# Hyena layers of a Trainium2 kernel: tokens split four ways, the filter's spectra taken a step ahead

## Chip, core and metric

The kernel runs on one core of a Trainium2 chip, in one launch. The metric is the device time in microseconds (us), the median of three runs. The engines are TensorE (PE), VectorE (DVE), ScalarE (ACT), GpSimd (POOL) and the DMA queues that SyncE (SP) and ScalarE issue.

## What is computed

A decoder of four layers (Hyena, window attention, pooling, Hyena, each with a feed-forward part) on 512 tokens of 1024 features, and behind it a second block with gated delta rule, latent attention and an MLP. The change touches the two Hyena layers alone:

```
def hyena_mixer(xn, ...):
    p = conv3(xn @ w_in + b_in)              # 3 x 1024 features, short convolution over tokens
    x1, x2, v = split(p)
    kf = rfft(hyena_filters(L, ...), axis=0) # 2 orders; taps forward and backward, times a decay,
                                             # divided by sum |k| over all taps
    z = v
    for o, gate in enumerate((x1, x2)):
        z = gate * (irfft(rfft(z, n=2 * L) * kf[:, o])[:L] + fbias[o] * z)
    return z @ w_out + b_out
```

## The kernel before

Each engine has its own program, written out by hand, and the programs meet through semaphores. `Tally` counts tiles in PSUM: four banks `acc` and four banks `aux` go round, and TensorE may open a tile only when the one four back has been drained (`acc_drained`, `aux_drained`). An engine takes its instructions strictly in the order of its program. All numbers are float32; a plain float32 matmul shows as two records in the trace. The large weight products are split in two rounded halves (`z_hi`, `z_lo`, and `out_hi` with the low half of the weights left in `ring_r`): three fast matmuls for one exact one. GpSimd makes the low half of the weights (`low_weights`, L806).

The long convolution is a product of spectra. It goes in four steps, `i = 0..3`: order `o = i // 2` and half `c = i % 2` of the 1024 features (512 each). In one step:

- TensorE makes the taps of the filter for the next step (`taps_of`, L1081, 8 matmuls); ScalarE copies them to `filt`, GpSimd multiplies them by the decay (L818, four instructions).
- TensorE transposes z to tokens in rows (L1036), in four groups of tokens; ScalarE copies them to `u_tm` (L1920).
- `spectra` (L1107): 8 tiles of two matmuls for the signal. Even and odd tokens apart give two tiles whose sum and difference are the two halves of a spectrum: ScalarE copies the even one to `tmpE` (L1965), VectorE adds and subtracts (L2553, L2554) into `U`. Behind them half of the filter's tiles, into `K` (which lies in `xn`).
- VectorE multiplies the spectra (`multiply`, L2563 to L2572): two quarters on 512 elements a partition, and a half on 1024.
- The inverse (L1057): 8 matmuls on 256 columns for each of four tiles of 128 features.
- VectorE scales by the filter's norm `invn`, adds the bias part `zbias` that ScalarE made and multiplies by the gate (L2534, L2536).
- The rest of the filter's spectra, and `magnitudes`: the larger of |fwd + bwd| and |fwd - bwd| (ScalarE L1894, VectorE L2486, L2487), whose column sums (L1097, 16 matmuls with one column) and reciprocal (L2495) give `invn`.

`K` holds one filter alone, so it is overwritten only when its products are done. In the last step the output product begins early: `first_half` (L990 to L992, 48 matmuls) stands on TensorE between the spectra and the inverse, and works on the first four tiles of z, whose low halves VectorE makes with `low_z` (L2491) ahead of that step's spectra. `second_half` (L999 to L1001, 48 matmuls) follows the inverse.

## Time and profile before

| | |
|---|---|
| median of 3 runs | 4452.16 us (4445.99 to 4461.49) |
| span of the profiled execution | 4437.2 us |
| own time of the profiled execution | not on its page; the span is what is shown of it |
| TensorE (PE) busy | 4169.9 us, 94% |
| VectorE (DVE) busy | 2225.3 us, 50% |
| GpSimd (POOL) busy | 1445.5 us, 33% |
| ScalarE (ACT) busy | 1236.0 us, 28% |

The span runs from the first to the last instruction. The busy shares are means over all stages; the Hyena layers' four steps each take some 237 us of the span, twice.

### The profile page before, as it was taken

Reading aid. Unit: us, or ns where it says so; the run is one execution under the profiler, and the core shown is the slowest. Engines: PE = TensorE matmul, PEld = TensorE weight load, DVE = VectorE, ACT = ScalarE, POOL = GpSimd, SP = SyncE. Lnnn points to the kernel's source line nnn. Section 1 sums busy time; section 2 is a strip of 40 time slices with the busy share of each in tenths; the row PEclk is TensorE's granted clock in tenths of the full one; section 3 lists DMA queues with packets and bytes.
Section 4 is the critical chain, followed back from the end, with each engine's and each line's share of the span. In section 5 each row is a group of like instructions: output and inputs, shape, how many; then the busy total and the mean of one; then the engine's idle time right before and its main releaser. Section 6 shows DMA issues by size and latency. Waiting matters only on the chain.

```text
span 4437.2 us, 48379 instructions
## 1 busy us (share of the span) xinstructions
PE 4169.9 (94%) x19126; PEld 3108.9 (70%) x19126; DVE 2225.3 (50%) x3267; ACT 1236.0 (28%) x1725; POOL 1445.5 (33%) x834
## 2 busy tenths in 40 slices
PE   7999999999999699999999999989998999998999
PEld 6656888656788488877557887566666666685887
DVE  6567435365424652465774444556663357404322
ACT  3322212135222322233233222322322224422221
POOL 3311344200344144434123442357574000231343
PEclk9999999999999899999999998989999879999999
DMA  6200232210232123221003222121212121221232
GB/s 181 76 16 23 111 105 88 105 48 28 101 115 77 70 96 118 81 77 67 28 29 131 99 90 68 43 60 31 60 30 57 59 77 60 74 95 62 90 105 76
DMA packets 96913, 333.75 MB, mean 75 GB/s; under 512 B 44336, under 2 KB 47536, under 8 KB 67888
## 3 DMA queue, kind: packets, MB, share of 16 engines
q1 hardware_dynamic: 87968, 311.85, 20.2%
q10 hardware_dynamic: 8720, 18.82, 1.7%
q8 instruction: 152, 2.49, 0.2%
q14 instruction: 73, 0.60, 0.0%
HBM read 317.53 MB, written 13.11 MB: 75 GB/s over the span
## 4 chain that ended last, share of the span: by engine, by line
PE 80%; DVE 14%; ACT 2%; POOL 2%; issue 1%; DMA 0%; SPq 0%; DVEq 0%; ACTq 0%; POOLq 0%
PE bank L903 16%; PE bank L904 16%; PE bank L905 16%; PE bank L1340 5%; PE bank L867 4%; PE bank L1107 3%; PE bank L1057 2%; PE bank L1320 1%; PE bank L1641 1%; PE bank L1081 1%; PE bank L1640 1%; PE bank L1662 1%; PE bank L1572 1%; PE bank L1601 1%; DVE work L2598 1%
## 5 line engine op out<-in xcount | busy, mean ns | idle before, releaser
L782 POOL TENSOR_TENSOR w_lo<-ring,w_hi 128x2048 fp32r<-128x2048 f32 (+2 forms) x200 | 777.2, 3886 | 1509.6 <-ACT w_hi L1777 1483.1
L903 PE MATMUL bank<-x_hi,w_hi 128*128 128x512 f32 x1584 | 618.2, 390 | 7.5 <-POOL w_lo L782 7.5
L905 PE MATMUL bank<-x_hi,w_lo 128*128 128x512 f32 x1584 | 616.9, 389 | 0.0
L904 PE MATMUL bank<-x_lo,w_hi 128*128 128x512 f32 x1584 | 616.7, 389 | 0.0
L1777 ACT ACTIVATE w_hi<-ring 128x2048 fp32r<-128x2048 f32 (+2 forms) x200 | 322.0, 1610 | 712.8 <-PE bank L905 711.9
L903 PE MATMUL bank<-h_hi,w_hi 128*128 128x512 f32 x960 | 373.9, 389 | 0.4
L904 PE MATMUL bank<-h_lo,w_hi 128*128 128x512 f32 x960 | 373.5, 389 | 0.0
L905 PE MATMUL bank<-h_hi,w_lo 128*128 128x512 f32 x960 | 373.4, 389 | 0.0
L903 PEld LDWEIGHTS bank<-x_hi,w_hi 128*128 128x128 f32 x1584 | 297.8, 188 | 70.6 <-POOL w_lo L782 9.2
L905 PEld LDWEIGHTS bank<-x_hi,w_lo 128*128 128x128 f32 x1584 | 297.6, 188 | 62.1
L904 PEld LDWEIGHTS bank<-x_lo,w_hi 128*128 128x128 f32 x1584 | 297.8, 188 | 61.5
L2420 DVE TENSOR_TENSOR x<-bank,x 128x512 f32<-128x512 f32 x72 | 49.8, 692 | 388.7 <-PE bank L905 347.5
L1340 PE MATMUL bank<-xn,ring 128*128 128x512 f32 x496 | 238.8, 620 | 1.4 <-DVE work L2741 1.4
L1107 PE MATMUL bank<-work,tab 128*128 128x512 f32 x512 | 225.8, 599 | 12.7 <-ACT work L1920 11.7
L795 POOL TENSOR_TENSOR ring_r<-ring,merge_hi 128x2048 fp32r<-128x2048 f32 x16 | 73.4, 4588 | 498.8 <-ACT merge_hi L2252 498.8
L903 PEld LDWEIGHTS bank<-h_hi,w_hi 128*128 128x128 f32 x960 | 180.2, 188 | 39.4 <-DVE h_lo L2357 2.1
L905 PEld LDWEIGHTS bank<-h_hi,w_lo 128*128 128x128 f32 x960 | 180.2, 188 | 37.4
L904 PEld LDWEIGHTS bank<-h_lo,w_hi 128*128 128x128 f32 x960 | 180.2, 188 | 37.3
L1107 PEld LDWEIGHTS bank<-work,tab 128*128 128x128 f32 x512 | 97.2, 192 | 131.8 <-issue 125.6
L1848 ACT ACTIVATE xn<-xn 128x512 f32<-128x512 f32 x88 | 55.7, 633 | 456.3 <-DVE xn L2433 456.3
L818 POOL TENSOR_TENSOR work<-work,ring 128x1024 f32<-128x1024 f32 x32 | 76.8, 2432 | 264.1 <-ACT work L1889 264.1
L2433 DVE TENSOR_TENSOR xn<-bank,rstd_t 128x512 f32<-128x512 f32 x88 | 60.9, 692 | 194.0 <-PE bank L905 187.3
(468 smaller groups left out, 7666.1 us busy)
## 6 DMA issues: line engine op xcount, KB each, us to landing
ring<-stream SPq DMA_DIRECT2D x212, 1024.0 KB, 4.8
ring<-stream SPq DMA_DIRECT2D x64, 704.0 KB, 4.0
ring<-stream SPq DMA_DIRECT2D x36, 512.0 KB, 3.6
xn<-first_mods SPq DMA_DIRECT2D x8, 1024.0 KB, 6.9
ring<-stream SPq DMA_DIRECT2D x4, 1088.0 KB, 5.0
bias_rows<-work ACTq DMA_DIRECT2D x1, 4096.0 KB, 46.4
work<-bias_rows ACTq DMA_DIRECT2D x1, 3072.0 KB, 11.2
tab<-tabs ACTq DMA_DIRECT2D x1, 2624.0 KB, 16.8
```

What stands on the lines that cost most here:

```text
L782: nc.gpsimd.tensor_tensor(w_lo[:, j % 2, 0:cols], ring[:, k % RING, 0:cols], w_hi[:, j % 2, 0:cols], ALU.subtract).then_inc(wlo_set, 1)
L795: nc.gpsimd.tensor_tensor(ring_r[:, w, 0:2 * DT * P], ring[:, w, 0:2 * DT * P], merge_whi[j % 2][:], ALU.subtract).then_inc(wlo_set, 1)
L818: nc.gpsimd.tensor_tensor(pair, pair, decay[:, pq:pq + 1, :].broadcast_to([P, 2, 512]), ALU.mult).then_inc(filt_set, 1)
L867: ins = mm(b[:], w[:, at + k, :], rhs[k] if isinstance(rhs, list) else rhs[:, k, :], start=(k == 0), stop=(k == kt - 1))
L903: mm(b[:], hi[:, at + k, :], rhs_hi, start=(k == 0), stop=False)
L904: mm(b[:], hi[:, at + k, :], rhs_lo[:, k, :], start=False, stop=False)
L905: ins = mm(b[:], lo[:, at + k, :], rhs_hi, start=False, stop=(k == kt - 1))
L1057: ins = mm(b[:, 256 * p:256 * (p + 1)], U[:, 4 * ft + 2 * kind + p, ct * P:(ct + 1) * P], inv[kind][:, p, ft, :], start=(j == 0), stop=(j ...
L1107: ins = mm(b[:], fwd[kind][:, p, q, ft * P:(ft + 1) * P], source(kind)[:, 2 * p + q, :], start=(q == 0), stop=(q == 1))
L1340: ins = mm(b[:, 0:TC] if ctx else b[:], w[:, at + k, :], src[:, k, :], start=(k == 0), stop=(k == DT - 1))
L1777: signal(go(w_hi[:, j % 2, 0:cols], ring[:, k % RING, 0:cols], ACT.Copy), whi_set)
L2433: drain(tt_(gate, bank(t)[:], rstd, ALU.mult), t)
```

## The change

Tokens are split four ways (token `4t + r`, `r = 0..3`) instead of two. A cosine or sine sum over one residue is one matmul (`FWD`, 12 blocks of 128x128), and sums and differences on VectorE build the spectrum:

- The signal's spectra are 8 matmuls instead of 16 (`signal_spectra`); VectorE builds four classes from them (`signal_pair`, `four_classes`). The filter's stay at 16, 8 tiles of two (`FILTER_PAIRS`).
- The inverse is 8 matmuls of 128 columns for each tile, in two parts: residues 0 and 2 when `prod_set` counts once, 1 and 3 when it counts again.
- The products are `crossed`, `straight`, `joined` and `folded`: VectorE instructions on 2048, 1536, 1024 and 512 elements, all 512 columns at once in steps 0 to 2, in two halves of 256 columns in step 3. Temporary products lie in `partner` (in `ctmp`), `cross` (in the table, which stays as large) and `cross3`.
- `K` is two buffers (`xn` and the new `spectrum2`). The next filter's spectra are made in the step before, between the products, and its taps one step earlier.
- `magnitudes` is two absolute values on ScalarE and one maximum on VectorE (L2535), which stands behind the products, ahead of the gates; its column sums stand behind the next step's signal spectra. The values lie in `x`, so ScalarE stores `x` to memory when the layer begins and loads it in step 3 (2 MB each).
- The output's first four low halves stand behind step 3's products in VectorE's order.

The diff, cut to what matters:

```
 pe:
+                for i in range(4):
+                    signal_spectra()
+                    if i:
+                        magnitudes()
                     if i < 3:
...
+                        filter_spectra()
+                        turns(i + 1)
                     else:
                         begun = first_half(0) + first_half(1)
...
+                    if i < 2:
+                        taps_of(i, later[1])
                     if i < 3:
...
+                        inverse(open_acc, acc_full, range(4))
+                    else:
+                        inverse(open_aux, aux_full, range(2))
+                        inverse(open_aux, aux_full, range(2, 4))
+                def signal_spectra():
...
+                    for pair in SIGNAL_PAIRS:
+                        for kind, r in pair:
+                            mm(open_aux()[:], fwd[kind, r, 1], u_tm[:, r, :], start=True, stop=True).then_inc(aux_full, 1)
+                def inverse_tile(b, ct, r):
+                    for k in range(2):
+                        ins = mm(b[:, P * r:P * (r + 1)], U[:, INVERSE_SLOTS[r][k], ct * P:(ct + 1) * P], inv[:, r, k, :],
+                                 start=(k == 0), stop=(k == 1))
+                def inverse(tiles_of, full_, cts):
+                    tiles = [tiles_of() for _ in cts]
+                    pe.wait_ge(prod_set, n["prod"] + 1)
...
+                    pe.wait_ge(prod_set, n["prod"] + 2)
 act:
+                    if i == 3:
+                        act.dma_start(x[:], x_keep.rearrange("(k p) t -> p k t", p=P)).then_inc(hy_x_back, 16)
                     if i < 3:
...
+                        magnitudes()
+                        spectra(4)
+                        turned()
+                    if i == 2:
+                        for j in range(2):
+                            high_weights(starts[("hyena", s)] + 18 + j, out_hi[j])
 dve:
+                    signal_pair(0, U[:, 0, :], U[:, 2, :])
...
+                    if i:
+                        norms(c)
                     if i < 3:
+                        whole = slice(0, 512)
+                        four_classes(whole)
+                        filter_pair(next_, 0)
+                        crossed(K[c], whole)
+                        filter_pair(next_, 1)
+                        straight(K[c], whole)
+                        filter_pair(next_, 2)
+                        joined(whole)
+                        filter_pair(next_, 3)
+                        folded(whole)
+                        magnitudes()
+                    else:
+                        for part in (slice(0, 256), slice(256, 512)):
+                            four_classes(part)
...
+                            folded(part)
...
                     if i == 3:
                         for m in range(4):
                             low_z(m)
+            def crossed(ker, cs):
+
+                tt_(partner[:, :, cs], U[:, 1:8:2, cs], ker[:, 1:8:2, cs], ALU.mult)
+                tt_(cross[:, :, cs], U[:, 0:6:2, cs], ker[:, 1:7:2, cs], ALU.mult)
+                step(tt_(cross3[:, :, cs], U[:, 6:7, cs], ker[:, 7:8, cs], ALU.mult))
+            def folded(cs):
+
+                low, high = U[:, 0:4, cs], U[:, 4:8, cs]
+                step(tt_(high, low, high, ALU.subtract))
+                step(stt(low, low, 2.0, high, ALU.mult, ALU.subtract))
+                first, second = U[:, 0:2, cs], U[:, 2:4, cs]
+                step(tt_(second, first, second, ALU.subtract))
+                signal(stt(first, first, 2.0, second, ALU.mult, ALU.subtract), prod_set)
```

The order of TensorE in step 1. L1081 are taps, L1036 transposes, L1107 spectra, L1057 the inverse, L1097 column sums. Before:

```order
L1081 MATMUL bank<-ring,work 128x512 x8
L1036 MATMUL bank<-ident,work 128x128 x16
L1107 MATMUL bank<-work,tab 128x512 x24
L1057 MATMUL bank<-tab,work 128x256 x32
L1107 MATMUL bank<-work,tab 128x512 x8
L1097 MATMUL bank<-ones,work 128x1 x16
```

In the changed kernel L1046 are the signal's spectra, L1143 the column sums, L1133 the filter's, L1037 the transposes of the next step, L1123 taps, L1050 the inverse:

```order
L1046 MATMUL bank<-work,tab 128x512 x8
L1143 MATMUL bank<-ones,x 128x1 x16
L1133 MATMUL bank<-work,tab 128x512 x16
L1037 MATMUL bank<-ident,work 128x128 x16
L1123 MATMUL bank<-ring,work 128x512 x8
L1050 MATMUL bank<-tab,work 128x128 x32
```

Taps and transposes moved behind the filter's spectra, so they stand next to the inverse; the column sums moved from the end of a step to the place behind the signal's spectra of the next.

The order of VectorE at the start of step 3. Before, the low halves L2491 follow the reciprocal L2495, ahead of the signal's pairs (L2553, L2554) and the products:

```order
L2495 RECIPROCAL small_t<-bank 128x4
L2491 TENSOR_TENSOR z_lo<-work,z_hi 128x512 x4
L2553 TENSOR_TENSOR work<-work,bank 128x512
L2554 TENSOR_TENSOR work<-work,bank 128x512
L2553 TENSOR_TENSOR work<-work,bank 128x512
L2554 TENSOR_TENSOR work<-work,bank 128x512
L2563 TENSOR_TENSOR work<-work,xn 128x512
```

In the changed kernel the end of the second half's products (L2638 to L2645) stands ahead of the same low halves, now L2539, and the gates (L2604) follow:

```order
L2638 TENSOR_TENSOR work<-work 128x4x256
L2639 SCALAR_TENSOR_TENSOR work<-work 128x4x256
L2641 TENSOR_TENSOR work<-work 128x2x256
L2642 SCALAR_TENSOR_TENSOR work<-work 128x2x256
L2644 TENSOR_TENSOR work<-work 128x2x256
L2645 SCALAR_TENSOR_TENSOR work<-work 128x2x256
L2539 TENSOR_TENSOR z_lo<-work,z_hi 128x512 x4
L2604 SCALAR_TENSOR_TENSOR work<-bank,small_t,work 128x512
```

The low halves moved from ahead of all of the step's products to behind them. TensorE's order there is unchanged: column sums, `first_half`, inverse, `second_half`.

## Rows read from the trace of the kernel before

**Rows 1.** The page's part 4, by line: shares of the span.
```profile
PE bank L903 16%; PE bank L904 16%; PE bank L905 16%; PE bank L1340 5%; PE bank L867 4%; PE bank L1107 3%; PE bank L1057 2%; PE bank L1320 1%; PE bank L1641 1%; PE bank L1081 1%; PE bank L1640 1%; PE bank L1662 1%; PE bank L1572 1%; PE bank L1601 1%; DVE work L2598 1%
```

**Rows 2.** Stretches of the first Hyena layer: us; busy PE, PEld, DVE, ACT, POOL; clock.
```profile
207.52:269.06 61.54, 56.10 (x193) 34.04 (x193) 40.89 (x51) 16.74 (x25) 9.31 (x5) 0.97 0.11 46
269.06:330.55 61.49, 56.04 (x192) 34.01 (x193) 40.89 (x51) 16.75 (x25) 9.30 (x5) 0.97 0.04 13
330.55:385.02 54.47, 49.63 (x177) 31.12 (x177) 40.89 (x51) 16.01 (x20) 7.49 (x3) 0.95 0.11 44
385.02:445.00 59.98, 55.16 (x194) 38.40 (x195) 47.60 (x51) 16.64 (x22) 11.42 (x3) 0.93 0.05 18
```

**Rows 3.** Timeline of TensorE, second step: start, length, engine, line, operation, count, wait.
```profile
269.06 20.84 PE L1107 MATMUL bank<-work,tab 128*128 128x512 f32 x48 [1.56 <-ACT work L1920]
291.26 7.17 PE L1057 MATMUL bank<-tab,work 128*128 128x256 f32 x32 [1.36 <-DVE work L2572]
...
316.48 3.63 PE L1097 MATMUL bank<-ones,work 128*128 128x1 f32 x32
```

**Rows 4.** Timeline of TensorE at the ends of both Hyena layers and the second's start.
```profile
441.13 0.40 PE L999 MATMUL bank<-z_hi,out_hi 128*128 128x512 f32 x1
...
444.63 0.39 PE L903 MATMUL bank<-z_hi,hyena_hi 128*128 128x512 f32 x1
...
2108.33 4.10 PE L1107 MATMUL bank<-work,tab 128*128 128x512 f32 x9 [1.56 <-ACT work L1920]
...
2343.01 0.39 PE L903 MATMUL bank<-z_hi,hyena_hi 128*128 128x512 f32 x1
```

**Rows 5.** TensorE's groups by form: count, then busy us and mean ns.
```profile
L1662 PE MATMUL bank<-work 128*128 128x128 f32 x384 | 49.2, 280 | 0.0
```

**Rows 6.** Timeline of VectorE in the second step.
```profile
291.24 1.22 DVE L2563 TENSOR_TENSOR work<-work,xn 128x1024 f32<-128x1024 f32 x1
...
300.94 0.69 DVE L2553 TENSOR_TENSOR xn<-work,bank 128x512 f32<-128x512 f32 x1
...
302.26 0.69 DVE L2553 TENSOR_TENSOR xn<-work,bank 128x512 f32<-128x512 f32 x1
...
305.96 2.29 DVE L2487 TENSOR_TENSOR work<-work 128x2048 f32<-128x2048 f32 x1
308.29 0.75 DVE L2534 SCALAR_TENSOR_TENSOR work<-bank,small_t,work 128x512 f32<-128x512 f32 x1
...
309.80 0.75 DVE L2534 SCALAR_TENSOR_TENSOR work<-bank,small_t,work 128x512 f32<-128x512 f32 x1
```

**Rows 7.** Timelines of GpSimd and VectorE: the decay of the second step.
```profile
261.30 9.30 POOL L818 TENSOR_TENSOR work<-work,ring 128x1024 f32<-128x1024 f32 x4 [52.23 <-ACT work L1889]
...
272.82 0.69 DVE L2553 TENSOR_TENSOR work<-work,bank 128x512 f32<-128x512 f32 x1 [13.90 <-PE bank L1107]
```

**Rows 8.** Timelines of GpSimd and VectorE where their instructions overlap.
```profile
163.78 10.51 POOL L818 TENSOR_TENSOR work<-work,ring 128x1024 f32<-128x1024 f32 x4 [2.09 <-ACT work L1889]
...
164.16 2.73 DVE L2480 SCALAR_TENSOR_TENSOR work<-work,vec 128x512 f32<-128x512 f32 x1
...
403.79 4.61 POOL L806 TENSOR_TENSOR ring_r<-ring,hyena_hi 128x2048 fp32r<-128x2048 f32 x1 [15.67 <-ACT hyena_hi L1789]
...
500.08 4.61 POOL L782 TENSOR_TENSOR w_lo<-ring,w_hi 128x2048 fp32r<-128x2048 f32 x1 [3.69 <-ACT w_hi L1777]
...
404.05 4.89 DVE L2563 TENSOR_TENSOR work<-work,xn 128x512 f32<-128x512 f32 x1
...
503.51 0.69 DVE L2433 TENSOR_TENSOR xn<-bank,rstd_t 128x512 f32<-128x512 f32 x1 [3.56 <-PE bank L905]
```

**Rows 9.** Timeline and stretch of TensorE after a wait in the first step.
```profile
239.42 8.86 PE L1057 MATMUL bank<-tab,work 128*128 128x256 f32 x32 [2.53 <-DVE work L2572]
...
239.40:243.00 3.60, 3.58 (x9) 2.89 (x10) 3.48 (x5) 0.00 (x0) 0.00 (x0) 0.53 0.00 0
```

**Rows 10.** DMA issues: count, size, us to landing.
```profile
x_keep<-x SPq DMA_DIRECT2D x1, 2048.0 KB, 8.5
```

More of the change, by code:

```diff
@@ L2544, in hyena @@
                 blk.n += 22
-            def spectra(dst, fts=(0, 1)):
-                for j in range(2 * fts[0], 2 * fts[-1] + 2):
-                    ft, kind = j // 2, j % 2
-                    e = aux.take()
-                    t = full(aux, aux_full)
-                    dve.wait_ge(aux_drained[aux.place(e)], aux.turn(e) + 1)
-                    tt_(dst[:, 4 * ft + 2 * kind, :], tmpE[:, j % 2, :], bank(t, True)[:], ALU.add)
-                    drain(tt_(dst[:, 4 * ft + 2 * kind + 1, :], tmpE[:, j % 2, :], bank(t, True)[:], ALU.subtract), t, True)
-                dve.wait_ge(aux_drained[aux.place(t)], aux.turn(t) + 1)
@@ new lines, in pair_tiles, with filter_pair, signal_pair @@
+            def pair_tiles(j):
+                e = aux.take()
+                t = full(aux, aux_full)
+                dve.wait_ge(aux_drained[aux.place(e)], aux.turn(e) + 1)
+                return tmpE[:, j % 2, :], bank(t, True)[:], t
+            def filter_pair(dst, j):
+                even, odd, t = pair_tiles(j)
+                tt_(dst[:, j, :], even, odd, ALU.add)
+                drain(tt_(dst[:, j + 4, :], even, odd, ALU.subtract), t, True)
+            def signal_pair(j, total, rest, flipped=False):
+                first, second, t = pair_tiles(j)
+                tt_(total, first, second, ALU.add)
+                drain(tt_(rest, second, first, ALU.subtract) if flipped else tt_(rest, first, second, ALU.subtract), t, True)
```

307 lines of the change are left out of this document (154 added, 153 removed).

## The prediction

> **What bounds the kernel now.** I read the chain that ended last first: the matmul lines of TensorE fill it, and the two lines of the transforms hold 3% and 2% of it [rows 1]. So the program waits for TensorE, and an edit in the two Hyena layers shows one for one in the span, if it moves the moment at which TensorE leaves the layer. Next the table of stretches, cut at the first signal spectrum of each of the four steps of the first Hyena layer: 61.5, 61.5, 54.5 and 60.0 us, TensorE busy 56, 56, 50 and 55 of them, VectorE 41, 41, 41 and 48 [rows 2]. TensorE bounds the steps, but VectorE is not far behind: halving TensorE's work can gain only until VectorE's column is reached. The timeline of TensorE in one step shows what lies in it: 24 spectra in 20.84 us, 7.17 us for half of the inverse and 3.63 us of column sums, with a short wait of 1.36 us for VectorE ahead of the inverse [rows 3].
>
> The second layer is a copy of this. It goes from the first signal spectrum at 2108.33 to the end of the first output block at 2343.01, 234.7 us; the first goes from 207.52 to 444.63, 237.1 us [rows 2, 4]. Together 471.8 us.
>
> **TensorE's new work.** A transform matmul on 512 columns costs 20.84/24 = 0.87 us [rows 3]. A step had 24 of them for spectra and 8 more behind the inverse; it now has 8 for the signal (7.0 us) and 16 for the filter (13.9 us). The inverse falls from 32 matmuls of 256 columns to 32 of 128. No such matmul is in this stage; elsewhere 384 records of 128x128 take 49.2 us, 0.13 us each, two records to a matmul [rows 5], so 32 cost 8.3 us for 14.3. The bounds are 7.2 (half of today's 14.3) and 14.3. With column sums (3.6) and eight taps (6.9) TensorE needs some 42 us, transposes included, of each of the first two steps, where it needed 56.
>
> **VectorE's new work.** From the timeline [rows 6]: a pair of sum and difference off a bank takes 302.26 - 300.94 = 1.32 us, an instruction on 2048 elements 2.32 us with its gap, one on 1024 a mean of 9.70/8 = 1.21 us inside a run and 1.25 with a wait behind it, a gate and its product 1.51 us. On 1536 I interpolate 1.76 us. The products of a step were 16 instructions on 512 and 8 on 1024, 20.6 us. They are now: four classes 2 x 2.3, crossed 4.7, straight 4.6, joined 4.7, folded 4.6 and then 4 x 1.23: 28.1 us. Pairs stay at 10.6, gates at 6.0, the maximum drops from 4.6 to 2.3. A step's sum is 47.2 us where it was 42: more work on VectorE, and VectorE becomes the engine that sets the step. No one price here is unknown by more than 1 us.
>
> **What moves under VectorE: GpSimd's instructions.** This decides the sign. GpSimd multiplies the taps by the decay in four instructions, 9.3 us, and today this lies in a hole of VectorE: the decay starts at 261.30 and VectorE stands idle 13.90 us before 272.82 [rows 7]. Where the two do overlap, VectorE's instruction does not run beside GpSimd's: the one at 164.16 takes 2.73 us during the decay, where an instruction of its form and size takes 0.75 us free [rows 6], and the one at 404.05 takes 4.89 us, to the end of the 4.61 us that GpSimd's instruction takes from 403.79, for 0.69 on 512 elements otherwise [rows 6, 8]. An instruction with a bank as operand is untouched: 0.69 us in the middle of a GpSimd instruction [rows 8]. And turns alternate: GpSimd's four decays took 10.51 us there and VectorE got one instruction through between two of them. So each GpSimd instruction costs VectorE 2.73 - 0.75 = 2.0 us (decay) or 4.89 - 0.69 = 4.2 us (weights).
>
> The Trainium skill, GPSIMD Engine Reference, section Specifications, says that GpSimd's SBUF interfaces are shared with VectorE, with contention for instructions with two SBUF inputs. The trace agrees (2.73 against 0.75 us). It does not say who gets the next turn. By alternating turns the sum is the one below; by VectorE always going first, it would be that of the first rival.
>
> In the changed order the taps stand behind the filter spectra and the transposes, whose last bank VectorE frees only after its last filter pair. The decay so begins under the folding: three of its instructions delay the second product signal (6.2 us) and one the maximum (2.0). In the third step there are no taps, but the two output-weight splits are issued at the same place: 8.4 us. Both were free before.
>
> **The chain by steps**, from the first signal spectrum (call it 0), "P" being the end of the folding:
> - P of step 0: signal 6.9 + last pair 1.6, four classes 4.6, four filter pairs 5.3, crossed, straight and joined 14.0, folding 9.5, GpSimd 6.2: 48.1.
> - From P to P in step 1: maximum 2.3 and GpSimd 2.0, gates 6.0, the first two signal pairs 2.6 (they free TensorE's banks), TensorE's last signal tile and column sums 0.87 + 3.63 and 0.5 of latencies, reciprocal 0.2, then again 4.6 + 5.3 + 14.0 + 9.5 + 6.2: 57.7. TensorE's own 42 us are hidden in it.
> - Step 2: the same with 8.4 for 6.2: 59.9. P is at 165.7.
> - Step 3: VectorE does maximum 2.3, waits until the inverse (begun at the first product signal, 2.5 before P) has its first tile at 4.8, gates 6.0, pairs 2.6, sums and latencies 5.0, reciprocal 0.2: 18.6 after P. Then the products in two halves, each 8 instructions on 1024 (9.7), 2 on 768 (1.9), 2 on 256 (0.8), 4 on 512 (2.9): 30.6 for both, and 4.2 for the weight split of GpSimd. Only behind them stand the first low halves of z: 54.1 after P.
> - TensorE's first output blocks wait for these and stand ahead of the last inverse. Before, low halves came first, and the 48 matmuls ((444.63 - 441.13)/15 = 0.233 us each, 11.2 us [rows 4]) lay under the products. Now TensorE is idle some 35 us, then 11.2, with 1.7 for half clock, inverse 8.3, first gates and z 1.5 to 2.0, and the other 48 matmuls 11.2: P + 89.
>
> Sum: 254.7 us a layer, 509.4 for two, against 471.8: +37.6. The start of the layer gives back 0.4 us twice (one maximum of 2.3 for two, one absolute value of 1.9 more). The half clock is from a row: after a wait of 2.53 us [rows 9] the granted clock was 0.53 for 3.6 us, so the lower level of 1.2 GHz, worth 1.7 us [rows 9]; elsewhere TensorE's waits lie in VectorE's shade. The two new copies of x lie beside other work: one like them lands in 8.5 us [rows 10], and its result is wanted only after eleven weight blocks on the way out and after step 3's products on the way back; without the cover 17 us a layer. The issue costs ScalarE half a microsecond. If it slows the first weight blocks I allow 0 to 4 us.
>
> So 4437.2 + 37 = 4474 us of span. The median of the runs, 4452.2, lies 15 us above this span; the profiled execution's own time is not on its page, so I add the same 15: 4489. A difference under 0.3%, 13 us, is about what a measurement of this kernel cannot tell from none.
>
> **Rivals.**
> 1. *GpSimd does not take turns; VectorE runs through.* For it: every overlap in the trace has VectorE arriving second or in short runs. Against it: at 403.79 GpSimd started within VectorE's chain, between two of its instructions. Then 29.0 us a layer go (16.4 of decays, 12.6 of splits); but TensorE's taps, 7 us behind the last pair, then end after the first product signal, the gates wait some 1.5 us for tiles, and the half clock falls on the inverse: 20 net. 4489 - 40 = 4449, the same as before. It decides when less than 1 us of each GpSimd instruction reaches VectorE.
> 2. *Faster: VectorE is fed without a wait too.* One mechanism: the tiles arrive a step ahead, as far as four banks allow, so that loop P to P is VectorE's 47.2. P of step 2 is 48.1 - 6.2 + 94.4 = 136.3, step 3 is 89 - 4.2: 221 a layer, -14.8 each: 4452 - 30 = 4422. Against it: the reciprocal stands in VectorE's order behind the signal pairs and needs column sums that TensorE starts only after the last signal tile; that is 5 us a step by order. It turns faster once stalls sum to less than 25 us a layer; I count 40.
> 3. *Much slower.* Each bank wait of TensorE (about 3.6 and 4 us before the last transposes) brings half clock onto the taps and the inverse, 3.4 us for three steps, and the copies delay weights 4: 4489 + 24 = 4513.
> 4. *The new parts don't shorten TensorE*: inverse at 14.3 instead of 8.3 us. Only step 3 and the end of step 2 show it: +12 a layer at most. 4489 + 24.
>
> **Chances.** The forecast, alternating turns and a last step that serialises, 0.64, own range 4470 to 4503. No turns 0.15. Something between (half the turns, 4469) 0.03. Faster 0.10. Rivals 3 and 4 together 0.08. The range leaves out the faster case and the slowest: 4446 to 4503, 8 in 10. Faster by over 0.3%: 0.11; within: 0.17; slower: 0.72.
>
> **What would show it.** In the new trace: signal spectra some 52, 58 and 63 us apart instead of 61.5, 61.5, 54.5; VectorE's 1024-element foldings of 3.2 us beside GpSimd's decays, and of 5.4 us beside the splits in the third step; TensorE idle about 35 us before the first output block, released by the low half of z; 82 us from the last step's spectra to the end of the first output block where it was 60. I am wrong if the foldings keep 1.2 us, if the output block starts under the products, or if steps 0 to 2 are all near 47.

## The result, and the profile after

The changed kernel takes 4522.84 us (median of four runs, 4507.8 to 4526.19) against 4454.77 for the kernel before in the same session: ratio 1.0150, 95% interval 1.0127 to 1.0173, so 68 us slower. The prediction was 4489 and its range ended at 4503, so the result lies outside it. The direction was right, the size about half of what came.

The page of the changed kernel, busy time by engine and the chain that ended last:

```profile
span 4524.4 us, 48077 instructions
...
PE 4107.8 (91%) x18998; PEld 3083.5 (68%) x18998; DVE 2313.3 (51%) x3227; ACT 1250.8 (28%) x1733; POOL 1461.1 (32%) x834
...
PE 78%; DVE 16%; issue 2%; POOL 2%; ACT 2%; ACTq 0%; DMA 0%; SPq 0%; DVEq 0%; POOLq 0%
```

TensorE does 62 us less work than before (4169.9) and the span is 87 us longer. In the chain that ended last, VectorE rose from 14% to 16% and TensorE fell from 80% to 78%: waits for VectorE took the place of transforms.

The stretches of the first Hyena layer, cut at the first signal spectrum of each step, columns as in [rows 2]:

```profile
229.12:280.68 51.56, 40.53 (x145) 24.16 (x146) 47.69 (x33) 17.21 (x24) 13.88 (x5) 0.90 0.13 55
280.68:342.21 61.53, 49.29 (x178) 29.81 (x177) 54.25 (x43) 18.65 (x26) 12.80 (x4) 0.83 0.10 35
342.21:409.63 67.42, 42.47 (x162) 26.76 (x161) 57.39 (x47) 18.41 (x21) 10.56 (x2) 0.75 0.04 15
409.63:491.00 81.37, 42.75 (x207) 33.05 (x206) 57.24 (x65) 17.29 (x23) 6.96 (x2) 0.75 0.11 39
```

Step 0 is 10 us shorter than before and step 1 unchanged. Steps 2 and 3 are 13 and 23 us longer (the last row is cut at 491.00; the output block ends at 491.88, so step 3 takes 82.3 us where it took 59.6). VectorE's column (the third busy time) now stands above TensorE's (the first) in all four rows. The granted clock (third from the end, as a share of full speed; 0.50 is the lower level of 1.2 GHz) is 0.75 to 0.90 where it was 0.93 to 0.97.

Where the 87 us between the two profiled spans lie, by the same landmarks in both traces: the first signal spectrum of the first layer comes 229.12 - 207.52 = 21.6 us later; from there to the end of the first output block the first layer takes 262.8 us against 237.1 (+25.7), the second 262.8 against 234.7 (+28.1); between and behind the layers lie another 5.4 and 6.4. That the medians differ by 68 and not 87 is because the profiled execution of before was some 15 us below its median and that of after 3 us above. For the start of the layer the prediction had 0 to 4 us, not 21.6. ScalarE's timeline there, its queue's issues (ACTq) with it:

```profile
37.07 0.66 ACTq L2350 DMA_DIRECT2D bias_rows<-work  x1
...
39.30 18.83 ACTq L1946 DMA_DIRECT2D x_keep<-x  x1
58.23 1.91 ACT L1825 ACTIVATE z_lo<-ring 128x2048 fp32r<-128x2048 f32 x1 [18.96 <-issue]
```

TensorE's timeline at the second weight block, and at the last sums and taps ahead of step 0:

```profile
64.77 0.79 PE L929 MATMUL bank<-x_hi_h,z_lo 128*128 128x512 f32 x1 [23.39 <-POOL ring_r L820]
...
211.71 4.73 PE L1143 MATMUL bank<-ones,x 128*128 128x1 f32 x32
216.30 9.36 PE L1123 MATMUL bank<-ring,work 128*128 128x512 f32 x16
```

The issue of the new store of x holds ScalarE's queue for 18.83 us; ScalarE's split of the second weight block waits behind it, GpSimd's half behind that, and TensorE stands still for 23.39 us, where before it waited 5.36 and began that block at 45.91. That is 18.9 of the 21.6 us. (The last two rows, column sums and taps, are 1.1 and 2.2 us longer than at full clock, 3.63 and 7.12 in the kernel before: this makes up the rest.) The same issue in the second layer took 0.37 us.

### The profile page after: what moved, and what is told of

The parts are those of the page before. It is cut to its first block, busy times and chain, and to the rows that moved or that the text cites. A ratio compares the mean times of both kernels' runs of the same rounds, so it can differ in the third digit from the quotient of the medians.

```text
span 4524.4 us, 48077 instructions
## 1 busy us (share of the span) xinstructions
PE 4107.8 (91%) x18998; PEld 3083.5 (68%) x18998; DVE 2313.3 (51%) x3227; ACT 1250.8 (28%) x1733; POOL 1461.1 (32%) x834
## 4 chain that ended last, share of the span: by engine, by line
PE 78%; DVE 16%; issue 2%; POOL 2%; ACT 2%; ACTq 0%; DMA 0%; SPq 0%; DVEq 0%; POOLq 0%
PE bank L929 16%; PE bank L930 16%; PE bank L931 16%; PE bank L1376 5%; PE bank L893 4%; PE bank L1356 1%; PE bank L1677 1%; PE bank L1133 1%; PE bank L1676 1%; PE bank L1698 1%; PE bank L1046 1%; PE bank L1608 1%; PE bank L1637 1%; PE bank L1123 1%; PE bank L1143 1%
## 5 line engine op out<-in xcount | busy, mean ns | idle before, releaser
L930 PEld LDWEIGHTS bank<-x_lo,w_hi 128*128 128x128 f32 x1584 | 297.7, 188 | 61.5
L838 POOL TENSOR_TENSOR work<-work,ring 128x1024 f32<-128x1024 f32 x32 | 90.6, 2861 | 228.1 <-ACT work L1925 228.1
L782 POOL TENSOR_TENSOR tab<-tab 56x31 f32<-56x31 f32 (+15 forms) x248 | 154.4, 622 | 19.4
L2761 DVE SCALAR_TENSOR_TENSOR kbuf<-xn,vec,kbuf 128x256 f32<-128x256 f32 x112 | 154.0, 1416 | 2.0
```

Of the source, the lines that this page charges most:

```text
L782: solve(tt(W[:, 0:i, i:SUB], W[:, 0:i, i:SUB], part, ALU.subtract))
L838: nc.gpsimd.tensor_tensor(pair, pair, factor[:, r:r + 1, :].broadcast_to([P, 2, 512]), ALU.mult).then_inc(filt_set, 1)
L930: mm(b[:], hi[:, at + k, :], rhs_lo[:, k, :], start=False, stop=False)
L2761: ins = stt(part, w[:, :, j, :], V("cond", 2 * j + c), part, ALU.mult, ALU.add)
```

## The experiments

Each result is told as the median, its ratio to the kernel before measured in the same session with the 95% interval, and the difference to that kernel in us; the changed kernel itself is at +68. A gain is told against this +68. Code is cut to what matters.

**1. Without the first store.** `s` is the number of the Hyena layer.

```
-                act.dma_start(x_keep..., x[:]).then_inc(hy_x_out, 16)
+                if s:
+                    act.dma_start(x_keep..., x[:]).then_inc(hy_x_out, 16)
...
+                        kept = x_keep if s else x_in
```

> The changed kernel, but the first Hyena layer doesn't store x: its x is the kernel's input, still in memory, and the layer reads that back behind step 3. The second layer stores and reloads as before. Theory (queue): in the trace of the changed kernel ScalarE's queue stood 18.83 us in the issue of this store, behind the 4096 KB of bias rows issued 1.6 us earlier, and the second block of the first layer's input weights began 18.9 us late. Without it that block starts near 46 us in place of 64.8, and the kernel takes 4504 us, 19 less. Rival (bandwidth): the store's 2 MB slow the weight blocks whoever issues them; then also about -19, which the next kernel tells apart. Rival (cover): TensorE would have waited there for other reasons, such as the decay or the bias rows, and gets back under 5 us.

Measured: 4497.74, ratio 1.0104 (1.0082 to 1.0127), +47: 21 us gone. The second block starts at 45.89, and the first signal spectrum comes 21.1 us earlier. The cost is on the path, whole.

**2. The store alone, in the kernel before.**

> The kernel before, with one thing added: the first Hyena layer's store of x, issued by ScalarE at the same place as in the changed kernel. Nothing reads what it stores. Theory (queue): 4455 + 19 = 4474 us, the issue takes 18 to 19 us on ScalarE, the second weight block starts near 65 us. Rival: the store alone costs under 5 us here, and the 19 us come only together with something else of the change, such as the smaller scratch for dynamic transfers.

Measured: 4466.88, ratio 1.0040 (1.0023 to 1.0056), +16. ScalarE's rows in it:

```profile
39.56 18.74 ACTq L1898 DMA_DIRECT2D x_keep<-x  x1
58.40 1.91 ACT L1790 ACTIVATE z_lo<-ring 128x2048 fp32r<-128x2048 f32 x1 [18.87 <-issue]
```

The same stall stands there with nothing else of the change, and with the scratch for dynamic transfers as it was: the rival falls. The 16 us of the medians (interval 10 to 25) agree with the 19 expected.

**3. The same two transfers in the other order.**

```
-                act.dma_start(x_keep..., x[:]).then_inc(hy_x_out, 16)
+                if s:
+                    act.dma_start(x_keep..., x[:]).then_inc(hy_x_out, 16)
...
+            act.dma_start(x_keep..., x[:]).then_inc(hy_x_out, 16)
             act.dma_start(scratch, brow...).then_inc(bias_rows_out, 16)
```

> The changed kernel with the first layer's store of x issued just ahead of the bias rows in place of 2 us behind them; the same bytes move, in the other order. Theory (queue): an issue stalls only when a large transfer of short packets stands ahead of it in the same engine's queue; the store has half the packets of the bias rows and nothing ahead of it, so its own issue takes under 1 us. Then either the issue of the bias rows stalls for less than the 18.8 us (it has only 2 MB ahead of it), and the second weight block starts between 46 and 60 us: 4500 to 4515 us; or it stalls as long, and nothing is won: 4523. Rival (bandwidth, weights slowed by the traffic): the second block starts at 64.8 in either order.

Measured: 4489.20 (4485.91, 4486.24, 4492.15 and once 4507.45), ratio 1.0087 (1.0059 to 1.0115), +37. Its issues, ScalarE's queue:

```profile
37.59 0.39 ACTq L2351 DMA_DIRECT2D x_keep<-x  x1
38.01 0.65 ACTq L2352 DMA_DIRECT2D bias_rows<-work  x1
```

Neither stalls, though the same bytes move, so it is no matter of bandwidth: the issue stalls when the 4096 KB of bias rows are ahead of it in its queue, and the 2048 KB of the store ahead do no harm. Whether the size or the pace of what stands ahead decides isn't separated: the store alone ahead lands in 7.4 us, the bias rows take 46. The gain of 31 us is more than the stall, and the stretches of the first layer say where the rest is:

```profile
208.91:260.46 51.55, 40.69 (x145) 23.98 (x145) 47.69 (x33) 17.21 (x24) 13.50 (x5) 0.90 0.13 54
260.46:318.17 57.71, 44.61 (x178) 27.04 (x177) 54.27 (x43) 18.66 (x26) 12.55 (x4) 0.91 0.11 38
318.17:380.87 62.70, 36.86 (x163) 23.53 (x161) 57.39 (x47) 18.43 (x21) 10.55 (x2) 0.81 0.04 16
380.87:463.10 82.23, 43.58 (x211) 33.58 (x210) 58.31 (x65) 17.60 (x23) 8.01 (x2) 0.75 0.11 39
```

The code of these steps is that of the changed kernel. VectorE is busy for the same 54.27 and 57.39 us, yet steps 1 and 2 take 57.7 and 62.7 us in place of 61.5 and 67.4, at a clock of 0.91 and 0.81 in place of 0.83 and 0.75. So the changed kernel loses 3.8 and 4.7 us with TensorE's clock. TensorE's timeline in step 1 of this kernel:

```profile
268.51 2.84 PE L1046 MATMUL bank<-work,tab 128*128 128x512 f32 x6 [1.78 <-DVE work L2666]
274.68 14.23 PE L1133 MATMUL bank<-work,tab 128*128 128x512 f32 x32
```

In the changed kernel the same two, behind the same waits of 1.55 and 1.78 us, take 4.54 and 16.73 us. Its stretches there, around the second of these waits, the last signal tiles and the start of the filter spectra:

```profile
285.00:289.00 4.00, 1.40 (x3) 0.57 (x4) 3.83 (x7) 1.55 (x4) 0.00 (x0) 1.00 0.00 0
289.00:293.00 4.00, 4.00 (x6) 1.54 (x6) 2.28 (x4) 0.98 (x2) 0.00 (x0) 0.57 0.00 0
297.00:299.00 2.00, 2.00 (x4) 1.02 (x5) 1.51 (x2) 1.57 (x1) 0.00 (x0) 0.50 0.00 0
```

So the clock falls behind the waits, ahead of the column sums, is at 1.00 again from 293 to 295 us, and falls a second time behind them. The same waits and the same work left it at 1.00 in the one kernel and not in the other; what differs is when the code arrives. I call this the phase; that it is the arrival alone that decides is argued from this, not shown. In the second layer the gain is smaller: 53.2, 58.2 and 62.0 us for steps 0 to 2, against 51.5, 61.5 and 67.4.

**4. GpSimd's decays cut short.**

```
-                        nc.gpsimd.tensor_tensor(pair, pair, factor[:, r:r + 1, :].broadcast_to([P, 2, 512]),
+                        few = pair[:, :, 0:8]
+                        nc.gpsimd.tensor_tensor(few, few, factor[:, r:r + 1, 0:8].broadcast_to([P, 2, 8]),
                                                 ALU.mult).then_inc(filt_set, 1)
```

> The changed kernel with a part left out: GpSimd multiplies only 8 of the 512 columns of each of the taps' tiles by the decay, so its 32 instructions of 2.0 to 3.2 us become short; nothing is moved. Theory (GpSimd's instructions take turns with VectorE's): the foldings of steps 0 and 1 fall from 3.2 to 1.2 us, steps 0 and 1 shorten by 6 to 8 us each, so 12 to 16 a layer; with the prologue's first decays, which nothing else of TensorE hides wholly, 0 to 5 more a layer: 4523 - 30 = 4493, range 4483 to 4499. Rival (no turns): VectorE's foldings keep their time for another reason, such as operands in two classes of rows: within 5 us of 4523.

Measured: 4490.53, ratio 1.0095 (1.0075 to 1.0114), +40: 28 us gone. Foldings of step 0 on VectorE's timeline, in the changed kernel:

```profile
267.09 3.28 DVE L2642 SCALAR_TENSOR_TENSOR work<-work 128x1024 f32<-128x1024 f32 x1
270.40 3.25 DVE L2644 TENSOR_TENSOR work<-work 128x1024 f32<-128x1024 f32 x1
```

And the same two with the decays cut short:

```profile
263.37 1.23 DVE L2643 SCALAR_TENSOR_TENSOR work<-work 128x1024 f32<-128x1024 f32 x1
264.63 1.23 DVE L2645 TENSOR_TENSOR work<-work 128x1024 f32<-128x1024 f32 x1
```

That is 2.0 us for each turn, as predicted. The total is as expected, its places aren't: steps 0 to 2 take 49.4, 53.5 and 60.4 us in both layers, so step 0 gives back only 2.2, step 1 8.0, and step 2, which has no decay, 7.0. Part of that is again the clock: in step 1 the filter spectra take 14.23 us here.

**5. GpSimd's instructions later, none left out.**

```
+                pool.wait_ge(gated, 16 * s + 4)
                 decay(2)
+                pool.wait_ge(gated, 16 * s + 8)
                 decay(3)
+                pool.wait_ge(gated, 16 * s + 12)
                 for b in range(4):
+                    if b == 2:
+                        pool.wait_ge(gated, 16 * s + 16)
                     low_weights(first + 18 + b, out_hi[b])
```

> The changed kernel, with GpSimd told to wait for the four gates of a step before it multiplies that step's taps by the decay (steps 0 and 1), before the first two splits of the output weights (step 2) and before the last two (step 3). The instructions are the same, only later, under VectorE's signal pairs, which read a bank. Theory (turns): the foldings take 1.2 us in steps 0 to 2, the first half of the products no 5.5 us; a step's end comes 6 to 8 us earlier. But the filter spectra then wait for the decay, whose last instruction ends 9 us behind the gates, and the maximum and column sums, which stand ahead of the spectra, wait 3.8 us more for ScalarE's absolute values: TensorE loses what VectorE wins. I expect a change within 10 us of 4523, 4517 the likeliest. Rival: the turns cost nothing on the path, and the delay alone shows: 4523 + 30 or more.

Measured: 4483.02, ratio 1.0064 (1.0045 to 1.0083), +30: 38 us gone where I expected 6. GpSimd's timeline in step 1:

```profile
282.44 9.29 POOL L838 TENSOR_TENSOR work<-work,ring 128x1024 f32<-128x1024 f32 x4 [52.21 <-DVE work L2610]
```

And the stretches of the first layer:

```profile
229.03:278.72 49.69, 40.22 (x145) 24.06 (x145) 42.45 (x37) 17.95 (x25) 1.20 (x1) 0.90 0.14 57
278.72:333.75 55.03, 45.57 (x178) 28.77 (x177) 46.42 (x43) 18.66 (x26) 9.29 (x4) 0.88 0.10 38
333.75:388.62 54.87, 39.33 (x163) 25.56 (x161) 47.34 (x43) 17.71 (x20) 9.28 (x4) 0.81 0.05 20
388.62:472.95 84.33, 45.81 (x211) 34.98 (x210) 59.03 (x65) 17.59 (x23) 17.53 (x4) 0.74 0.11 38
```

The four decays take 9.29 us, the free 2.3 each, in place of 12.8, and VectorE's busy time falls from 54.3 and 57.4 to 46.4 and 47.3: nearly nothing collides. My reason against it was wrong: the filter spectra wait only 0.82 us for the decay, and the maximum ahead of the sums is of the filter before this one. Step 0 gains 1.9 us only, because VectorE, ready earlier, waits 3.28 us for TensorE's taps and inverse. Step 3 loses 2: a split now falls beside two low halves, which take 5.62 us in place of 1.49.

Not all of the 38 us is the turns. Steps 1 and 2 of the changed kernel ran in a bad phase of the clock. Beside the kernel of experiment 3, whose GpSimd order is the old one, steps 0 to 2 are 12.4 us shorter in the first layer (159.6 against 172.0) and 14.5 in the second, and step 3 is 2 longer in each: 23 us for both layers are the turns, and the rest came with the clock. VectorE's work fell by more, by 7.8 us in step 1 where the step itself fell by 2.7: without the turns it is no longer VectorE alone that sets the steps.

**6. The first low halves ahead of step 3's products.**

```
                     if i:
                         norms(c)
+                    if i == 3:
+                        for m in range(4):
+                            low_z(m)
...
-                    if i == 3:
-                        for m in range(4):
-                            low_z(m)
                     for ct in range(4):
```

> The changed kernel, with the high and low halves of the first four rows of z made ahead of step 3's products: on ScalarE behind the copies of step 3's signal tiles, on VectorE behind the reciprocal. Nothing else moves. Theory (the last step serialises): TensorE's 48 matmuls of the first halves, 11.2 us and 1.6 of half clock, then lie under the products, for 2.9 us of VectorE that now stand ahead of them: -10 to -12 a layer, 4523 - 22 = 4501 us; TensorE no longer stands idle some 36 us in one piece, and from step 3's first signal spectrum to the end of the first output block it is near 71 us instead of 81.3. Rival: the products slow down by as much, since the halves are read from memory beside them, or the inverse is late for another reason: within 3 us of 4523.

Measured: 4481.83, ratio 1.0073 (1.0055 to 1.0091), +31: 37 us gone. TensorE's timeline at the first output block, in the changed kernel:

```profile
456.71 0.76 PE L1016 MATMUL bank<-z_hi,out_hi 128*128 128x512 f32 x1 [35.76 <-DVE z_lo L2539]
```

With the low halves early, the same block and what follows it:

```profile
416.19 0.58 PE L1016 MATMUL bank<-z_hi,out_hi 128*128 128x512 f32 x1 [1.16 <-DVE z_lo L2540]
...
451.46 6.62 PE L1050 MATMUL bank<-tab,work 128*128 128x128 f32 x32 [9.44 <-DVE work L2643]
457.84 0.48 PE L1025 MATMUL bank<-z_hi,out_hi 128*128 128x512 f32 x1
```

From the last step's first signal spectrum to the end of the block it is 67.8 us in place of 82.3, 14.4 in each layer: the products hid the first 48 matmuls, and of the inverse only the second half is left behind them. The other 8 us come with the clock: step 1 takes 58.2 us in both layers, step 2 keeps 67.5 in the first and takes 62.1 in the second, and the first layer starts 2.7 us earlier.

**7. ScalarE's order.** One copy of a signal tile moved ahead of the last scaled row of the step before:

```
                     for ct in range(2, 4):
                         scaled_rows(i, ct)
+                        if i < 3 and ct == 2:
+                            spectra(1)
```

> The changed kernel; on ScalarE the copy of each step's first signal tile stands ahead of the last scaled row of the step before, so it doesn't wait for the second gate. Theory (ScalarE's order makes TensorE wait and so brings half clock onto the filter spectra): TensorE's wait of 1.55 us before its ninth signal tile goes, steps 1 and 2 shorten from 61.5 and 67.4 to 58 and 64: 4523 - 12 = 4511. Rival (the half clock has other causes, the banks that VectorE frees late): steps 1 and 2 stay within 1.5 us, 4523 - 2, within noise.

Measured: 4509.16, ratio 1.0126 (1.0106 to 1.0147), +57, the time I expected, and yet the theory isn't borne out: steps 1 and 2 of the first layer kept 61.5 and 67.3 us. TensorE's two waits of 1.55 and 1.78 us became one:

```profile
285.79 4.54 PE L1046 MATMUL bank<-work,tab 128*128 128x512 f32 x6 [3.29 <-DVE work L2666]
290.16 4.51 PE L1143 MATMUL bank<-ones,x 128*128 128x1 f32 x32
```

The second layer took 58.2 and 62.0 with the same wait, shorter (1.97 us). The gain lies in the second layer's steps 1 and 2 and at the start of the first (2.9 us), though the edit is the same in both layers: most likely phase again, which isn't shown. A total that agrees proves nothing.

**8. Fillers: is it the waits that lower the clock?** Matmuls that compute nothing, into the next free bank:

```
+                def filler(count):
+                    t = acc.n
+                    pe.wait_ge(acc_drained[acc.place(t)], acc.turn(t))
+                    for _ in range(count):
+                        mm(bank(t)[:], ident[:], TB("fwd")[:, 0:512], start=True, stop=True)
```

> The changed kernel with matmuls added that compute nothing: identity by a constant table into the next free bank, 5 and 9 of them ahead of the second and fourth transposes of steps 1 to 3, 3 ahead of the fifth and of the seventh signal tile, 2, 2 and 32 ahead of the inverses of steps 0 to 2 and 80 in TensorE's wait ahead of the first output block, each 0.43 us at full clock and about the length of the waits that are there. Theory (steps 1 and 2 were 4 us longer than the sum of their parts because TensorE, after its waits, ran signal tiles, sums and spectra at half clock): the filter spectra take 13.9 us in place of 16.7 and the sums 3.6 in place of 4.2 in both layers, steps 1 and 2 take 57.7 and 60 to 63 us in both, and the inverses of step 2 7.4 in place of 9.9: 9 us a layer, 4523 - 18 = 4505, with 1.7 a layer more at the output blocks. Rival (the 4 us are ScalarE's order of copies, whatever the clock): steps 1 and 2 keep 61.5 and 67.4.

Measured: 4618.74, ratio 1.0372 (1.0353 to 1.0392), +161. I had the filler's length wrong: it is a float32 matmul of two records, 0.86 us, so every wait got twice its length. But it showed what no other kernel could: TensorE without a gap. Its stretches around the sums of step 1:

```profile
270.00:289.30 19.30, 19.30 (x93) 12.47 (x92) 14.45 (x15) 3.80 (x6) 8.65 (x3) 1.00 0.00 1
289.30:293.80 4.50, 4.50 (x33) 4.46 (x32) 1.29 (x2) 0.03 (x1) 0.00 (x0) 0.77 0.00 0
293.80:298.50 4.70, 4.70 (x7) 2.12 (x8) 4.38 (x3) 4.37 (x3) 0.00 (x0) 0.50 0.01 3
298.50:310.00 11.50, 11.50 (x28) 5.04 (x28) 10.24 (x10) 1.84 (x4) 0.00 (x0) 1.00 0.00 0
```

Busy in full, the clock at 1.00, then the column sums (32 records of one column), and behind them the lower level of 1.2 GHz for 5 us, on the filter spectra. No wait was there. Two more kernels, with fillers of the right length, the second with short sums:

```
-                    for r in range(4):
-                        ins = mm(b[:, ct:ct + 1], mags[:, r, ct * P:(ct + 1) * P], ones[:, 0:1], ...
+                    for r in range(1):
```

> The kernel with fillers, corrected in length: a filler takes 0.86 us of TensorE, not 0.43, so there are now 3 and 5 ahead of the second and fourth transposes, 2 ahead of the fifth and seventh signal tiles, 16 ahead of the third inverse and 40 ahead of the first output block. Theory A (waits pull the clock down): with its waits filled TensorE has full clock and steps 1 and 2 take 57.7 and 60 to 63 us in both layers: 4523 - 18 = 4505. Theory B (the column sums do, 32 matmuls of one column in 3.6 us: in the kernel with long fillers TensorE was never idle and its clock still fell to 0.50 behind them, at 293 us, for 5 us): the spectra behind them keep 16 us and steps 1 and 2 stay near 61.5 and 66, so 4520 or, where the fillers delay something, up to 4535.

> The same kernel, with a part left out: the column sums take only one of the four classes of rows, 4 matmuls in place of 16. The maximum and all else stay. Theory B (column sums pull the clock down): the spectra behind them fall from 16.3 to 13.9 us in both layers and steps 1 and 2 shorten by the 2.7 us of sums left out, and 2.5 to 4 more each: 16 to 20 us below the kernel with all four classes. Theory A (waits): only the 2.7 us of each of the four sums on the path go, 10 to 12 us, and spectra of 16 us stay where they were.

Measured: 4512.06, ratio 1.0131 (1.0113 to 1.0149), +60, and 4486.12, ratio 1.0068 (1.0045 to 1.0091), +34. The sums of step 1 on TensorE's timeline, with all four classes, and the stretch behind them:

```profile
292.89 4.19 PE L1155 MATMUL bank<-ones,x 128*128 128x1 f32 x32
```

```profile
297.00:303.00 6.00, 6.00 (x9) 2.61 (x9) 4.68 (x3) 4.42 (x3) 0.00 (x0) 0.53 0.00 0
```

The same with short sums:

```profile
285.62 0.95 PE L1155 MATMUL bank<-ones,x 128*128 128x1 f32 x8
```

```profile
286.40:292.00 5.60, 5.60 (x15) 2.58 (x15) 5.50 (x6) 4.51 (x4) 0.00 (x0) 1.00 0.00 0
```

With the full sums and no wait near them the spectra of steps 1 and 2 take 16.8 and 16.7 us in the first layer and 15.5 and 15.7 in the second; with short sums they take 14.2 in all four, and the clock stays at 1.00. By the clock theory B holds: the sums are a cause of their own.

The times agree less. 4512 lies between the 4505 of theory A and the 4520 of B. From full to short sums it is 26 us, where B said 16 to 20 and A 10 to 12. Steps 1 and 2 shorten by 4.3 us each in the first layer and 2.6 in the second, of which the sums' own length is 2.7; B had 2.5 to 4 more in each. So what the sums take through the clock is 1.6 us a step in the one layer and nothing in the other, and it is at most a part of the 3.8 and 4.7 us of experiment 3. Most of the rest of the 26 us lies ahead of the layers' first signal spectra (7.3 and 4.0 us), where a column sum stands too.

Open is what decides. Behind full sums of 3.63 us the clock stayed at 1.00 in the kernel before, in steps 1 and 2 of the first layer of experiment 3, and in step 2 of the second layer in the kernel with long fillers. The work ahead of the sums doesn't tell them apart: in the first of these kernels 7 us of spectra stand there, and in the changed kernel's prologue 14 us of spectra stand ahead of sums behind which the taps ran at 0.50.

**9. Everything behind the gates, and the sums too.** The first-layer store left out as in 1, the edits of 5 and 6, and:

```
-                    if i:
-                        magnitudes()
                     if i < 3:
                         filter_spectra()
+                        magnitudes()
                         turns(i + 1)
```

The maximum and the reciprocal move on VectorE as the expectation says.

> The changed kernel with four things together: no store of x in the first layer; the first low halves ahead of step 3's products; GpSimd's decays and output splits behind the gates; and the column sums of the next filter moved behind its spectra, with the maximum on VectorE behind the second filter pair and the reciprocal behind the fourth, so that neither the sums nor the reciprocal stand ahead of the products. Theory (VectorE then bounds the steps at its own 47 us, with one or two turns left beside the four classes): steps 0 to 2 take 45, 51 and 50 us, step 3 to the end of the first output block 65: some 212 us behind the first signal spectrum, 25 less a layer than before the change, and 4455 - 40 = 4415 us for the whole, faster than both kernels. Rival (TensorE or GpSimd is late by the decay: filter spectra wait for it, and the half clock stays): steps of 56 to 58 us, 4450 to 4465.

Measured: 4462.05, ratio 1.0022 (1.0012 to 1.0032), +9. The rival held, by its mechanism and its time. TensorE in step 1:

```profile
275.55 16.73 PE L1137 MATMUL bank<-work,tab 128*128 128x512 f32 x32 [7.24 <-POOL work L838]
```

With the sums moved away nothing lies between the signal tiles and the filter spectra, so TensorE waits 7.24 us for a decay that used to be covered by the sums; the steps take 53.0, 61.5 and 59.6 us, where the rival had 56 to 58 each. The clock is low on the spectra here too (0.50 from 275.5 to 281 us), behind this wait and with no sums ahead, so both causes exist.

**10. Three edits together** (3, 5 and 6), and **11.** the same with the taps ahead of the transposes on TensorE.

> The changed kernel with three of the single edits together: the store of x ahead of the bias rows, the first low halves ahead of step 3's products, GpSimd's decays and output splits behind the gates. Measured alone they gave 34, 41 and 40 us. In the traces the start of the first layer gained 19 by the first, the last step 14 a layer by the second, steps 0 to 2 some 20 a layer by the third; the rest of the single gains is full TensorE clock in steps 1 and 2, which only one of them can give. Theory (the costs add, apart from that clock): 4523 - 19 - 28 - 40 = 4436, range 4430 to 4446, which is faster than the kernel before (4453). Rival (they cover each other: the output splits, now late, hold back the first halves that were moved forward): step 3 keeps 75 us or more and the time is 4452 or above.

> The kernel with the three edits, and one more: on TensorE the eight taps of steps 0 and 1 stand ahead of the transposes in place of behind them, on ScalarE likewise. They need nothing of VectorE, so they fill the 2.4 and 4.7 us that the transposes wait for banks. Theory (in the kernel with late decays the chain of steps 0 and 1 runs from VectorE's last filter pair over the last transposes, 8.1 us of taps and the inverse to the gates, for which VectorE waits 3.3 and 2.9 us): these waits go, steps 0 and 1 take 46.5 and 52 us, 6 us a layer: 12 us below the kernel with three edits. Rival: VectorE's wait goes, but the first gate then waits for the inverse's own 7.4 us behind the product signal: under 3 us in all.

Measured: 4431.08 against 4457.42, ratio 0.9951 (0.9936 to 0.9967), 26 us faster than the kernel before; and 4429.18, ratio 0.9947 (0.9932 to 0.9962), which the runs can't tell from it. Stretches of the first of them:

```profile
207.83:257.82 49.99, 40.48 (x145) 24.07 (x146) 42.45 (x37) 17.93 (x25) 0.92 (x1) 0.90 0.14 56
257.82:313.07 55.25, 45.52 (x178) 28.51 (x177) 46.71 (x43) 18.65 (x26) 9.29 (x4) 0.88 0.10 38
313.07:367.98 54.91, 39.36 (x162) 25.60 (x161) 47.35 (x43) 17.70 (x20) 9.29 (x4) 0.81 0.06 20
367.98:438.90 70.92, 49.75 (x211) 38.91 (x210) 59.04 (x65) 17.59 (x23) 17.53 (x4) 0.81 0.13 45
```

It is 231 us to the end of the first output block, where the changed kernel took 262.8 and the kernel before 237.1. The gains nearly add: 31 + 38 + 37, so 106 one by one, and 94 together. Each single edit had also brought steps 1 and 2 a better phase of the clock, and this gain can be had only once, which the expectation had allowed for. The taps' new place shortened step 0 by 1.7 us and step 1 by 0.5: TensorE's 0.95 us waits went, but the inverse then waited 6.5 us for VectorE's products; the rival's side.

## Why the prediction was right, and where it failed

The mechanism of the steps held. What failed are two terms of the sum: the price of the store's issue, and the half clock outside the last step.

- **VectorE sets the steps**: right. The four steps at 51.6, 57.7, 62.7 and 82.1 us (experiment 3, first layer) sum to 254.0, in the second layer to 255.7; the prediction said 254.7. This is its mechanism, step by step, when TensorE's clock is up on the signal tiles and filter spectra. The inverse was priced 1 us too long (8.3 us, measured 7.3), which is within what the steps agree to.
- **Alternating turns with GpSimd**: right in size, 3.25 us beside a decay and 5.40 beside a split, as VectorE's timeline of the third step has it:

```profile
388.92 5.41 DVE L2641 TENSOR_TENSOR work<-work 128x1024 f32<-128x1024 f32 x1
394.37 5.40 DVE L2642 SCALAR_TENSOR_TENSOR work<-work 128x1024 f32<-128x1024 f32 x1
```

  The first rival put the net worth of all turns at 40 us. Taking them away without leaving work out gave 38, but only some 23 of it are the turns (experiment 5), so the agreement is in part luck. The Trainium skill, GPSIMD Engine Reference, section Specifications, has the shared interfaces for instructions with two SBUF inputs; the traces agree (3.25 against 1.23 us). That section doesn't say who goes next; these rows do: one instruction of each engine after the other.
- **The last step serialises**: right. TensorE idle 35.76 us before the first output block (predicted some 35); undoing it gave 14.4 us a layer.
- **Failed: "The issue costs ScalarE half a microsecond ... I allow 0 to 4 us."** No row stood behind the half microsecond. It cost 18.8 us in ScalarE's queue in the first layer. I took the price of an issue from free queues and asked how long the transfer takes to land, not what stands ahead of it. The trace of before had the row, in its view of the DMA queues from 30 to 100 us, which the prediction didn't use:

```profile
bias_rows<-work ACTq DMA_DIRECT2D x1, 4096.0 KB, 46.4
```

  The new store is issued 1.6 us behind the end of this issue in the same queue, while the transfer has some 44 us to go. The Trainium skill, DMA: Bandwidth & Descriptors, section Issuing engines are not separate DMA queues, says that the time on the sequencer to start a transfer is usually small relative to the transfer; the 0.37 us of the second layer agree, the 18.83 us here don't.
- **Failed: "elsewhere TensorE's waits lie in VectorE's shade."** The half clock was charged once a layer, 1.7 us. It also fell on the last signal tiles, the sums and the filter spectra of steps 1 and 2, for which VectorE waits, and cost 3.8 and 4.7 us there, 8.5 a layer when the phase is bad. The column sums can bring it about as well as waits do, which the prediction had no thought of. The third rival had half clock on the taps and the inverse, and 24 us; it named the right kind and the wrong place.
- The start of the layer, forecast at -0.4 us, lost 2.7 to the same clock. Between and behind the layers 11.8 us were lost in code that the change doesn't touch. The kernel of experiment 2, which is the kernel before in these stretches, took 3.8 and 3.9 us longer there than the profile of before; so most of it comes without the change. That it is phase is argued, not shown.

Together, in the profiled spans: 37 us predicted, 18.9 for the issue, 2 x 8.5 for the clock in steps 1 and 2, 3 at the start and 11.8 elsewhere make 88, where 87 were measured. The two slow rivals were priced at 24 us for all such mishaps together, and the range left them out; the stall of the issue was in none of the rows that the prediction was built on. That experiment 3 lands on the forecast time, 4489, is partly luck: it has the issue's cost taken out and the better phase.

## What to carry to other kernels

Before a DMA is added to an engine that also computes, look at what its queue is still moving at that moment. The issue itself can stall and take the engine's compute with it; here swapping two issues cost nothing and saved 19 us. GpSimd's instructions with two SBUF inputs were best started where VectorE works out of PSUM; a wait on a semaphore moved them there and gave 38 us, some 23 of them without the gain in clock. And where a change leaves gaps and thin matmuls on TensorE, compare the granted clock of stretches before believing that an edit did what its total says.

## What the runs showed of the hardware

- The issue of a 2048 KB store stood 18.83 and 18.74 us behind 4096 KB of broadcast rows in ScalarE's queue (the changed kernel, experiment 2); ahead of them it took 0.39 us, and the broadcast itself 0.65 (experiment 3).
- Behind 32 matmul records of one column TensorE's granted clock fell to 0.50 with no gap before it (experiment 8, step 1), though not everywhere; behind eight such records it stayed at 1.00 in all four steps looked at.
- VectorE's instruction with two SBUF inputs on 1024 elements took 3.25 us beside GpSimd's decay and 5.40 beside its split, for 1.23 free.
- The same code took 61.5 or 57.7 us for a step, at a granted clock of 0.83 or 0.91. A kernel's runs spread likewise, the longer ones at a lower mean clock: 4485.91 us at 0.939 and 4507.45 at 0.935, 4507.8 at 0.936 and 4526.19 at 0.933.
